# Conformer convolution module: gate tiles, layer-norm root and second product reordered, with the root on GpSimd

## The chip, the cores and the metric

The kernel runs on one core of a Trainium2 chip. The metric is the device time of one execution in microseconds (us), lower is better. Five engines work side by side and meet only at semaphores: TensorE (PE, whose weight loads are PEld), VectorE (DVE), ScalarE (ACT), GpSimd (POOL) and SyncE (SP), which issues the DMAs.

## The reference, cut to what matters

A two-layer hybrid decoder step; only the token mixer of layer 0 is touched, a causal Conformer convolution module over 1,104 tokens (64 of the sample group, 1,040 of the prompt) of width 1,024:

```python
def conformer_conv(h, hist, w_pw1, b_pw1, w_dw, b_dw, ln_g, ln_b, w_pw2, b_pw2):
    u = h @ w_pw1 + b_pw1
    g = u[..., :D_CONV] * jax.nn.sigmoid(u[..., D_CONV:])
    gh = jnp.concatenate([hist.astype(g.dtype), g], axis=1)
    new_hist = gh[:, -CONV_HIST:]
    c = causal_dwconv(gh, w_dw, b_dw)
    c = jax.nn.silu(layernorm(c, ln_g, ln_b))
    return c @ w_pw2 + b_pw2, new_hist
...
    y = xc * lax.rsqrt(jnp.mean(xc * xc, axis=-1, keepdims=True) + EPS)
```

The rest (RMS norms, two SwiGLU feed-forwards, the Mamba-2 mixer of layer 1) is the same in both kernels.

## The kernel before, in words

Tokens lie in three chunks of 368 columns (`TC`, `NC` = 3), model width in eight tiles of 128 (`KT` = 8). A dense product of one output tile and one chunk is 24 matmuls (`dense`: eight k-tiles, each as three fp32r products of high and low parts). Weights come in units of 128 x 1,024 into two slots; ACT splits off the high part (`split`, L1038), POOL the low part (L1763).

**First product (`pw1`).** For each of the eight tiles m there are two units, v = 0 (the linear half, PSUM banks 0 to 2) and v = 1 (the gate, banks 3 to 5). ACT takes the sigmoid chunk by chunk (`gates`, L1105), DVE multiplies (`glu_tile`, L1386 and L1387). PE then turns the finished gate tile of the tile before into rows of time (`turn_gates`, 14 transposes in four sets, through banks 6 and 7), and ACT keeps the four sets in `gt` (`keep_gates`, L1119). Sets 2 and 3 use the same banks as sets 0 and 1, so they wait until ACT has kept those.

**Windows.** The convolution is done by a discrete Fourier transform on 14 windows (`WIN`; 97 tokens each for ten of the prompt and 70 for its last, three small ones of 24, 24 and 16 tokens for the sample group, which come fifth to seventh in `ORDER`). Window x is a step: PE analyses (`analyse`, L664), DVE multiplies by the spectrum of the filter (`products`, L1408 and L1409), PE synthesizes (`synthesize`, L674 and L675), ACT keeps the sums (`keep_sums`, L1128), DVE takes mean and variance (`stats`, L1417 and L1419). PE runs its analysis two windows ahead.

**Layer norm.** ACT takes the root of the variances in three groups (`roots`, L1134: windows 0 to 6, 7 to 9, 10 to 13), DVE inverts it (`inverses`, L1425) and normalises (`normalise`, L1431). PE turns the window back (`turn_back`, 8 transposes), ACT applies gain, bias and silu and splits off the high part (`silus`, L1143 and L1147), POOL the low part (L1793). The table `BEHIND` says behind which step this tail of a window is done: window 0 behind step 7, and only windows 0 to 8 inside the loop of steps.

**Second product (`pw2_first`).** Chunk 0 needs windows 0 to 6, chunk 1 windows up to 9, chunk 2 all; in PE's queue the turns of window 9 and of windows 10 to 13 stand between the chunks. The loop over the other six output tiles follows.

The order of each engine's queue is the order of its block in the code; nothing else schedules.

Of the kernel before, what the change touches and what calls it, by code (L numbers as in the profile page):

```python
# [26 lines left out]
ACT = mybir.ActivationFunctionType  # L27
# [3 lines left out]
P = 128  # L31
# [92 lines left out]
def hybrid_step(nc, i, o):  # L124
    with ExitStack() as ctx:
# [29 lines left out]
        with ExitStack() as conv_scope:  # L155
            def cb(name, shape):
                return conv_scope.enter_context(nc.sbuf_tensor(name, shape, F32))

            wspec = cb("wspec", [P, 2, D])
            tab_k = cb("tab_k", [P, K_END])  # L160
            wrow = cb("wrow", [P, D])
            bst = cb("bst", [P, 2, 12])
            mv = cb("mv", [P, WIN, 2])
            rstd = cb("rstd", [P, WIN])
        ahi = sb("ahi", [P, 2, T], F32R)
# [16 lines left out]
        def chunk_buffer(start):  # L182
# [101 lines left out]
        ws_mm, ws_kept, x_done, t_ready, c_done, c_kept, c_stat = (sem(x) for x in (  # L284
            "ws_mm", "ws_kept", "x_done", "t_ready", "c_done", "c_kept", "c_stat"))
        ln_step, ln_aggr, ln_root, ln_inv, cn_ready, tb_done, y_silu, l_hi, l_lo = (sem(x) for x in (
            "ln_step", "ln_aggr", "ln_root", "ln_inv", "cn_ready", "tb_done", "y_silu", "l_hi", "l_lo"))
# [87 lines left out]
        LN_GROUPS = [(0, 7), (7, 10), (10, WIN)]  # L375
        LN_OF = [n for n, (a, b) in enumerate(LN_GROUPS) for _ in range(a, b)]
        BEHIND = {7: [0], 8: [1], 9: [2], 10: [3], 11: [4, 5], 12: [6, 7], 13: [8]}
# [187 lines left out]
        def _(pe):  # L565
# [65 lines left out]
            def pw1(m):  # L631
                for v in range(2):
                    unit_ready(U_PW1 + 2 * m + v)
                    for c in range(NC):
                        pe.wait_ge(g_glu, NC * m - 2 + c)
                        dense(3 * v + c, v, FULL, xhi, xlo, c)

            def turn_gates(m, a):

                pe.wait_ge(g_glu, NC * m + NC)  # L640
                G = glu[a]
                for n, (w0, w1) in enumerate(SETS):
# [12 lines left out]

            def analyse(x):

                w, n, col, kd, k1, k2 = window(x)
                if x == 4:
                    pe.wait_ge(in_hist, 16 * SWN)  # L660
                for half in range(2):
                    pe.wait_ge(gt_kept, 4 * (3 if half == 0 else 7) + SET_OF[w] + 1)
                    wait(pe, t_ready, 2 * (x - 2) + half + 1)
                    pe.matmul(bank[2 * (x % 2) + half][:, :], tab_k[:, kd:kd + P], gt[:, w, half * 512:half * 512 + 512],  # L664
                              start=True, stop=True).then_inc(x_done, 1)
# [26 lines left out]
            pw1(1)  # L692
            turn_gates(0, 0)
            with pe.Fori(1, KT // 2) as m2:
                pw1(2 * m2)
                turn_gates(2 * m2 - 1, 1)
                pw1(2 * m2 + 1)
                turn_gates(2 * m2, 0)
# [10 lines left out]
            def pw2_first(c):  # L709

                pe.wait_ge(l_lo, (7, 10, WIN)[c])
                for v in range(2):
                    if c == 0:
                        unit_ready(U_PW2 + v)
                    dense(3 * v + c, v, FULL, xhi, xlo, c)
# [317 lines left out]
        def _(act):  # L1033
# [77 lines left out]
            def keep_gates(m):  # L1111

                for n, (w0, w1) in enumerate(SETS):
# [15 lines left out]

            def roots(r):  # L1130

                a, b = LN_GROUPS[r]
                act.wait_ge(ln_aggr, b)
                act.activation(rstd[:, a:b], mv[:, a:b, 1], ACT.Sqrt, bias=eps[:, 0:1]).then_inc(ln_root, 1)  # L1134
# [217 lines left out]
        def _(dve):  # L1352
# [43 lines left out]
            def products(x):  # L1396
# [4 lines left out]
                for half in range(2):  # L1401
                    hs = slice(half * 512, half * 512 + 512)
                    dve.wait_ge(x_done, 2 * x + half + 1)
# [17 lines left out]
            def inverses(r):  # L1421

                a, b = LN_GROUPS[r]
                dve.wait_ge(ln_root, r + 1)
                dve.reciprocal(rstd[:, a:b], rstd[:, a:b]).then_inc(ln_inv, 1)  # L1425

            def normalise(x):

                w, n, col, kd, k1, k2 = window(x)
                dve.wait_ge(ln_inv, LN_OF[x] + 1)  # L1430
# [287 lines left out]
        def _(pool):  # L1718
# [71 lines left out]
            for x in range(WIN):  # L1790
# [3 lines left out]
                                   ALU.subtract).then_inc(l_lo, 1)  # L1794
            for m in range(KT - 2):
# [121 lines left out]
```

## Time and profile before

| what | value |
|---|---|
| median of 3 runs | 3596.91 us (3589.69 to 3606.87) |
| the profiled execution: its time, its span | 3604.03 us, 3602.3 us |
| PE, PEld busy | 3355.0 us (93%), 3180.7 us (88%) |
| DVE, ACT, POOL busy | 1385.1, 894.1, 892.4 us |
| mean granted TensorE clock | 0.969 of full speed |

The span is what the profiler records between the first and the last instruction of the core. PE is busy for nearly all of it, so a change can gain only where PE stands still or runs at its lower clock. The stretch that the change touches lies between 115 and 454 us.

### The profile page before, as it was taken

Reading aid. Unit: us, or ns where it says so; the run is one execution under the profiler, and the core shown is the slowest. Engines: PE = TensorE matmul, PEld = TensorE weight load, DVE = VectorE, ACT = ScalarE, POOL = GpSimd, SP = SyncE. Lnnn points to the kernel's source line nnn. Section 1 sums busy time; section 2 is a strip of 40 time slices with the busy share of each in tenths; the row PEclk is TensorE's granted clock in tenths of the full one; section 3 lists DMA queues with packets and bytes.
Section 4 is the critical chain, followed back from the end, with each engine's and each line's share of the span. In section 5 each row is a group of like instructions: output and inputs, shape, how many; then the busy total and the mean of one; then the engine's idle time right before and its main releaser. Section 6 shows DMA issues by size and latency. Waiting matters only on the chain. (4 is left out here: it accounts for less than half of the span.)

```text
span 3602.3 us, 51683 instructions
## 1 busy us (share of the span) xinstructions
PE 3355.0 (93%) x19814; PEld 3180.7 (88%) x19814; DVE 1385.1 (38%) x2358; ACT 894.1 (25%) x1621; POOL 892.4 (25%) x662
## 2 busy tenths in 40 slices
PE   4999798999999995979999999999987999999998
PEld 3896597999999994969999889999877999999997
DVE  4004323222223236354645556464555222322234
ACT  2212622111111112323333233333322111111112
POOL 2311223121212112323232333333233121121210
PEclk8999899999999997999999999999999999999999
DMA  3111011111111110101111120111110111111111
GB/s 100 36 35 28 1 39 38 42 42 45 41 47 41 47 47 16 42 26 54 38 36 44 44 60 21 54 38 36 48 39 18 48 41 47 41 45 42 44 43 56
DMA packets 226515, 148.43 MB, mean 41 GB/s; under 512 B 7474, under 2 KB 208274, under 8 KB 226320
## 3 DMA queue, kind: packets, MB, share of 16 engines
q1 hardware_dynamic: 226360, 146.31, 13.7%
q8 instruction: 104, 1.70, 0.2%
q14 instruction: 51, 0.42, 0.0%
HBM read 131.56 MB, written 15.44 MB: 41 GB/s over the span
## 5 line engine op out<-in xcount | busy, mean ns | idle before, releaser
L575 PE MATMUL bank<-xhi,whi 128*128 128x368 f32 x3840 | 1293.5, 337 | 94.0 <-issue 33.0
L575 PE MATMUL bank<-xlo,whi 128*128 128x368 f32 x3840 | 1282.9, 334 | 0.0
L575 PE MATMUL bank<-xhi,wlo 128*128 128x368 f32 x3840 | 1279.3, 333 | 0.0
L1763 POOL TENSOR_TENSOR wlo<-stage,whi 128x1024 fp32r<-128x1024 f32 x220 | 537.1, 2442 | 1728.8 <-ACT whi L1038 1728.8
L575 PEld LDWEIGHTS bank<-xhi,whi 128*128 128x128 f32 x3840 | 733.9, 191 | 113.6 <-issue 58.2
L575 PEld LDWEIGHTS bank<-xlo,whi 128*128 128x128 f32 x3840 | 733.1, 191 | 2.7
L575 PEld LDWEIGHTS bank<-xhi,wlo 128*128 128x128 f32 x3840 | 733.1, 191 | 0.0
L1502 DVE TENSOR_TENSOR h<-h,bank 128x368 f32<-128x368 f32 x528 | 284.2, 538 | 720.6 <-PE bank L575 720.6
L575 PE MATMUL bank<-ahi,whi 128*128 128x368 f32 x1440 | 495.2, 344 | 4.3 <-DVE alo L1483 3.8
L575 PE MATMUL bank<-alo,whi 128*128 128x368 f32 x1440 | 477.4, 332 | 0.0
L575 PE MATMUL bank<-ahi,wlo 128*128 128x368 f32 x1440 | 476.9, 331 | 0.0
L1038 ACT ACTIVATE whi<-stage 128x1024 fp32r<-128x1024 f32 x220 | 231.3, 1053 | 587.1 <-PE bank L575 552.6
L575 PEld LDWEIGHTS bank<-ahi,whi 128*128 128x128 f32 x1440 | 271.8, 189 | 8.4 <-DVE alo L1483 4.4
L575 PEld LDWEIGHTS bank<-alo,whi 128*128 128x128 f32 x1440 | 271.8, 189 | 2.7 <-issue 0.3
L575 PEld LDWEIGHTS bank<-ahi,wlo 128*128 128x128 f32 x1440 | 271.6, 189 | 0.0
L1491 DVE TENSOR_TENSOR arena<-arena,bank 128x368 f32<-128x368 f32 x132 | 71.1, 538 | 464.5 <-PE bank L575 464.5
L567 PE MATMUL bank<-ident,arena 128*104 128x128 f32 (+7 forms) x934 | 145.0, 279 | 82.6 <-DVE arena L1666 20.0
L567 PEld LDWEIGHTS bank<-ident,arena 128*104 128x104 f32 (+7 forms) x934 | 107.5, 149 | 113.8 <-issue 40.3
L1199 ACT ACTIVATE ahi<-arena 128x368 fp32r<-128x368 f32 x132 | 67.6, 512 | 446.1 <-DVE arena L1491 446.1
L1608 DVE SCALAR_TENSOR_TENSOR arena<-arena,params 128x1040 f32<-128x1040 f32 x96 | 169.8, 1769 | 0.0
L1187 ACT ACTIVATE arena<-bank 128x368 f32<-128x368 f32 x132 | 62.5, 479 | 398.3 <-PE bank L575 398.2
L1326 ACT ACTIVATE arena<-bank,arena 104x104 f32<-104x104 f32 (+1 forms) x352 | 92.4, 344 | 246.0 <-PE bank L881 245.8
(196 smaller groups left out, 2800.6 us busy)
## 6 DMA issues: line engine op xcount, KB each, us to landing
stage<-in_ssd_w_in SPq DMA_DIRECT2D x48, 512.0 KB, 4.2
stage<-in_ffn_w_gate SPq DMA_DIRECT2D x44, 512.0 KB, 3.8
stage<-in_ffn_w_up SPq DMA_DIRECT2D x44, 512.0 KB, 3.7
stage<-in_ffn_w_down SPq DMA_DIRECT2D x44, 512.0 KB, 3.5
stage<-in_cf_w_pw SPq DMA_DIRECT2D x24, 512.0 KB, 4.0
arena<-in_state_ssm SPq DMA_DIRECT2D x16, 512.0 KB, 4.8
out_ss_s<-arena SPq DMA_DIRECT2D x16, 512.0 KB, 3.2
stage<-in_ssd_w_out SPq DMA_DIRECT2D x16, 512.0 KB, 3.5
```

Source lines behind the costliest of these rows:

```text
L567: return pe.transpose(out, in_, ident[0:k, 0:k])
L575: mm = pe.matmul(bank[b][:, 0:TC], w[:, slot, w0:w0 + P], x[:, k, cs], start=n == 0, stop=n == 3 * len(offs) - 1)
L1038: act.activation(whi[:, slot, :], stage[:, slot, :], ACT.Copy).then_inc(w_hi, 1)
L1187: act.activation(sg[:, j, c * TC:(c + 1) * TC], bank[3 * j + c][:, 0:TC], ACT.Silu)\
L1199: act.activation(ahi[:, j, c * TC:(c + 1) * TC], actv[q % 2], ACT.Copy).then_inc(f_hi, 1)
L1326: a = act.activation(dec[0:l, q * l:(q + 1) * l], bc_bank[0:l, q * l:(q + 1) * l], ACT.Exp, bias=tab[0:l, NACS, c, q:q + 1])
L1491: dve.tensor_tensor(actv[q % 2], sg[:, j, c * TC:(c + 1) * TC], bank[q][:, 0:TC], ALU.mult)\
L1502: dve.tensor_tensor(hm, hm, bank[q % 6][:, 0:TC], ALU.add).then_inc(f_down, 1)
L1608: dve.scalar_tensor_tensor(op, rp[:, t:t + NP_], w, op, ALU.mult, ALU.add).then_inc(r_step, 1)
L1763: pool.tensor_tensor(wlo[:, slot, :], stage[:, slot, :], whi[:, slot, :].bitcast(F32), ALU.subtract)\
```

## The change

Four edits go together. (1) `turn_gates` and `keep_gates` take a list of sets: sets 0 and 1 of the tile before are turned between the two halves of a tile's first product, sets 2 and 3 behind the second half, and the last tile's sets are interleaved with the first analyses (for which `x_done` becomes one semaphore for each half). (2) The root moves from ACT to POOL: `inverse_root` does it for each window by six small operations on a column of one element a partition (add epsilon, power of -0.5, one Newton step), each behind a wait on the one before; ACT's `roots` and DVE's `inverses` are gone. (3) The tail of window x - 1 (normalise, turn back, silu, split) is done behind step x, for all windows. (4) The second product starts behind the loop of steps, with the last window's turn between its first two halves.

```diff
-        LN_GROUPS = [(0, 7), (7, 10), (10, WIN)]
...
-        BEHIND = {7: [0], 8: [1], 9: [2], 10: [3], 11: [4, 5], 12: [6, 7], 13: [8]}
...
-            def pw1(m):
+            def pw1(m, a):
+
                 for v in range(2):
                     unit_ready(U_PW1 + 2 * m + v)
                     for c in range(NC):
                         pe.wait_ge(g_glu, NC * m - 2 + c)
                         dense(3 * v + c, v, FULL, xhi, xlo, c)
-
-            def turn_gates(m, a):
+                    turn_gates(m - 1, a, (2 * v, 2 * v + 1))
+
+            def turn_gates(m, a, sets):
...
-            turn_gates(KT - 1, 1)
-            analyse(0)
-            analyse(1)
+            analyse(0, 0)
+            turn_gates(KT - 1, 1, (0, 1))
+            analyse(1, 0)
+            turn_gates(KT - 1, 1, (2, 3))
+            analyse(0, 1)
+            analyse(1, 1)
             for x in range(WIN):
                 synthesize(x)
                 if x + 2 < WIN:
-                    analyse(x + 2)
-                for y in BEHIND.get(x, ()):
-                    turn_back(y)
+                    analyse(x + 2, 0)
+                    analyse(x + 2, 1)
+                if x:
+                    turn_back(x - 1)
...
-            pw2_first(0)
-            turn_back(9)
+            pw2_first(0, 0)
+            turn_back(WIN - 1)
+            pw2_first(0, 1)
             pe.wait_ge(c_kept, 2 * WIN)
-            pw2_first(1)
-            for x in range(10, WIN):
-                turn_back(x)
-            pw2_first(2)
+            for c in (1, 2):
+                for v in range(2):
+                    pw2_first(c, v)
...
-            gates(1, 1, False)
-            keep_gates(0)
+            keep_gates(0, (0, 1))
+            gates(1, 1, False)
+            keep_gates(0, (2, 3))
             with act.Fori(1, KT // 2) as m2:
-                gates(2 * m2, 0, False)
-                keep_gates(2 * m2 - 1)
-                gates(2 * m2 + 1, 1, False)
-                keep_gates(2 * m2)
-            keep_gates(KT - 1)
+                for a in range(2):
+                    m = 2 * m2 + a
+                    keep_gates(m - 1, (0, 1))
+                    gates(m, a, False)
+                    keep_gates(m - 1, (2, 3))
+            keep_gates(KT - 1, (0, 1, 2, 3))
             for x in range(WIN):
                 keep_sums(x)
-                if x == 6:
-                    roots(0)
-                elif x == 9:
-                    roots(1)
-                for y in BEHIND.get(x, ()):
-                    silus(y)
-            roots(2)
-            for x in range(9, WIN):
-                silus(x)
+                if x:
+                    silus(x - 1)
+            silus(WIN - 1)
...
                 if x + 1 < WIN:
                     products(x + 1)
-                if x in (7, 11):
-                    inverses(x // 8)
-                for y in BEHIND.get(x, ()):
-                    normalise(y)
+                if x:
+                    normalise(x - 1)
                 stats(x)
-            normalise(9)
-            inverses(2)
-            for x in range(10, WIN):
-                normalise(x)
+            normalise(WIN - 1)
...
+            def inverse_root(x):
+
+                w, n, col, kd, k1, k2 = window(x)
+                ve, r0_, sq, e, half_ = (root[0:n, j:j + 1] for j in range(5))
+                pool.wait_ge(ln_aggr, x + 1)
+                rstep(pool.tensor_scalar(ve, mv[0:n, x, 1:2], EPS, None, ALU.add))
+                rstep(pool.tensor_tensor(r0_, ve, half_, ALU.pow))
+                rstep(pool.tensor_tensor(sq, r0_, r0_, ALU.mult))
+                rstep(pool.tensor_tensor(sq, sq, ve, ALU.mult))
+                rstep(pool.tensor_scalar(e, sq, -0.5, 1.5, ALU.mult, ALU.add))
+                pool.tensor_tensor(rstd[0:n, x:x + 1], r0_, e, ALU.mult).then_inc(ln_inv, 1)
...
+            for x in range(WIN):
+                inverse_root(x)
+                if x:
+                    low_part(x - 1)
+            low_part(WIN - 1)
```

**PE, end of the first product.** Before, from the last gate tile's four turns (banks 6 and 7) to the first synthesis:

```order
L567 MATMUL bank6<-ident,arena 127x128 x4
L567 MATMUL bank7<-ident,arena 127x128 x4
L567 MATMUL bank6<-ident,arena 127x128 x3
L567 MATMUL bank7<-ident,arena 24x128 x3
L664 MATMUL bank0<-arena,tab_k 128x512
L664 MATMUL bank1<-arena,tab_k 128x512
L664 MATMUL bank2<-arena,tab_k 128x512
L664 MATMUL bank3<-arena,tab_k 128x512
L674 MATMUL bank4<-arena,tab_k 97x512
```

The same place of the changed kernel (a transpose is L566 there, an analysis L667, the first matmul of a synthesis L677):

```order
L667 MATMUL bank0<-arena,tab_k 128x512
L566 MATMUL bank6<-ident,arena 127x128 x4
L566 MATMUL bank7<-ident,arena 127x128 x4
L667 MATMUL bank2<-arena,tab_k 128x512
L566 MATMUL bank6<-ident,arena 127x128 x3
L566 MATMUL bank7<-ident,arena 24x128 x3
L667 MATMUL bank1<-arena,tab_k 128x512
L667 MATMUL bank3<-arena,tab_k 128x512
L677 MATMUL bank4<-arena,tab_k 97x512
```

The two analyses of the first half (banks 0 and 2) now stand where PE otherwise waits for ACT to empty banks 6 and 7.

**PE, one step of the windows.** Step 1 of the loop in the kernel before, up to the start of step 2:

```order
L674 MATMUL bank4<-arena,tab_k 97x512
L675 MATMUL bank4<-arena,tab_k 97x512
L674 MATMUL bank5<-arena,tab_k 97x512
L675 MATMUL bank5<-arena,tab_k 97x512
L664 MATMUL bank2<-arena,tab_k 128x512
L664 MATMUL bank3<-arena,tab_k 128x512
```

And of the changed kernel (L678 is the second matmul of a synthesis):

```order
L677 MATMUL bank4<-arena,tab_k 97x512
L678 MATMUL bank4<-arena,tab_k 97x512
L677 MATMUL bank5<-arena,tab_k 97x512
L678 MATMUL bank5<-arena,tab_k 97x512
L667 MATMUL bank2<-arena,tab_k 128x512
L667 MATMUL bank3<-arena,tab_k 128x512
L566 MATMUL bank6<-ident,arena 128x97 x4
L566 MATMUL bank7<-ident,arena 128x97 x4
```

The turn of window 0 stands in step 1; before, it stood in step 7.

**POOL, the stretch of the windows.** Before, between the splits of weights (`wlo`) there is only the low part of each window (L1793):

```order
L1763 TENSOR_TENSOR wlo<-stage,whi 128x1024 x14
L1793 TENSOR_TENSOR xlo<-arena,xhi 128x8x97 x4
L1793 TENSOR_TENSOR xlo<-arena,xhi 128x8x24 x2
L1793 TENSOR_TENSOR xlo<-arena,xhi 128x8x16
L1793 TENSOR_TENSOR xlo<-arena,xhi 128x8x97 x6
L1793 TENSOR_TENSOR xlo<-arena,xhi 128x8x70
```

The changed kernel, one window's root and the low part of the window before it (L1796):

```order
L1785 TENSOR_SCALAR root<-mv 97x1
L1786 TENSOR_TENSOR root<-root 97x1
L1787 TENSOR_TENSOR root<-root 97x1
L1788 TENSOR_TENSOR root<-root 97x1
L1789 TENSOR_SCALAR root<-root 97x1
L1790 TENSOR_TENSOR rstd<-root 97x1
L1796 TENSOR_TENSOR xlo<-arena,xhi 128x8x97
```

Six small operations for each of 14 windows (84 in all) now stand in POOL's queue between the low parts.

## Rows read from the trace of the kernel before

**Rows 1.** Windows view: busy us of each engine, PE's granted clock (PEclk), DMA.

```profile
114.79:306.17 191.38, 183.16 (x1093) 180.75 (x1093) 12.91 (x27) 35.36 (x58) 39.12 (x14) 0.99 0.12 36
306.17:316.92 10.75, 8.92 (x38) 5.67 (x37) 2.96 (x6) 5.52 (x10) 2.35 (x1) 0.84 0.13 29
316.92:382.48 65.56, 65.56 (x177) 25.28 (x175) 50.22 (x89) 33.20 (x66) 6.59 (x4) 1.00 0.07 18
382.48:401.49 19.01, 14.89 (x50) 6.67 (x49) 9.62 (x16) 12.64 (x39) 3.47 (x5) 0.73 0.00 1
401.49:453.75 52.26, 35.23 (x194) 33.52 (x193) 7.56 (x13) 24.99 (x59) 12.19 (x8) 0.77 0.00 0
```

**Rows 2.** Groups of instructions, PE, 114.79 to 306.1 us: busy, mean ns | idle before.

```profile
L567 PE MATMUL bank<-ident,arena 128*127 128x128 f32 (+1 forms) x84 | 12.2, 281 | 8.0 <-ACT arena L1119 8.0
```

**Rows 3.** Timeline, PE, one block of gate turns: start, duration, [idle before <- releaser].

```profile
171.08 0.99 PE L567 MATMUL bank<-ident,arena 128*127 128x128 f32 x6 [1.32 <-ACT arena L1119]
```

**Rows 4.** Timeline, ACT, the sets of the last two gate tiles.

```profile
307.91 1.07 ACT L1119 ACTIVATE arena<-bank 127x512 f32 x2
309.34 0.87 ACT L1119 ACTIVATE arena<-bank 127x384 f32 x2 [0.36 <-PE bank L567]
```

**Rows 5.** Timeline, PE, starts of steps 0, 7, 9 and 10, and step 9's parts.

```profile
316.92 1.02 PE L674 MATMUL bank<-arena,tab_k 128*97 128x512 f32 x2
...
353.89 1.02 PE L674 MATMUL bank<-arena,tab_k 128*97 128x512 f32 x2
...
365.53 1.02 PE L674 MATMUL bank<-arena,tab_k 128*97 128x512 f32 x2
...
368.96 1.88 PE L664 MATMUL bank<-arena,tab_k 128*128 128x512 f32 x4
370.68 0.83 PE L567 MATMUL bank<-ident,arena 97*128 97x97 f32 x8
371.35 1.02 PE L674 MATMUL bank<-arena,tab_k 128*97 128x512 f32 x2
```

**Rows 6.** Timeline, DVE, step 9's statistics and what follows them.

```profile
369.56 1.29 DVE L1417 BATCH_NORM_STATS2 bst<-arena 97x6 f32<-97x512 f32 x2 [1.22 <-ACT arena L1128]
370.88 0.21 DVE L1419 BATCH_NORM_AGGREGATE mv<-bst 97x2 f32<-97x12 f32 x1
371.01 0.64 DVE L1408 TENSOR_TENSOR arena<-bank,wspec 128x512 f32<-128x512 f32 x1
...
373.36 0.81 DVE L1431 TENSOR_SCALAR arena<-arena,mv,rstd 97x1024 f32<-97x1024 f32 x1
```

**Rows 7.** Timeline, ACT, one window's silu and the next sums kept.

```profile
365.39 2.70 ACT L1143 ACTIVATE arena<-bank,params 128x97 f32<-128x97 f32 x8 [1.27 <-PE bank L567]
...
368.88 1.06 ACT L1128 ACTIVATE arena<-bank 97x512 f32<-97x512 f32 x2
```

**Rows 8.** Timeline, POOL: small operations of the setup, and one low part.

```profile
5.01 0.31 POOL L1749 TENSOR_TENSOR upto_s<-same_s,upto 64x64 f32<-64x64 f32 x1
5.42 0.24 POOL L1751 TENSOR_SCALAR cut_s<-upto_s 64x64 bf16<-64x64 f32 x1
...
369.06 1.69 POOL L1793 TENSOR_TENSOR xlo<-arena,xhi 128x776 fp32r<-128x776 f32 x1 [4.12 <-ACT xhi L1147]
```

**Rows 9.** Groups of instructions, PE, 316.92 to 453.75 us.

```profile
L575 PE MATMUL bank<-xhi,whi 128*128 128x368 f32 x49 | 18.4, 375 | 11.1 <-POOL xlo L1793 11.1
...
L567 PE MATMUL bank<-ident,arena 97*128 97x97 f32 (+3 forms) x112 | 13.9, 263 | 10.0 <-ACT arena L1143 9.2 <-DVE arena L1431 0.8
```

**Rows 10.** Timeline, DVE: what the second product's chunk 2 releases, half by half.

```profile
449.76 0.60 DVE L1464 SCALAR_TENSOR_TENSOR h<-bank,params,h 128x368 f32<-128x368 f32 x1 [20.63 <-PE bank L575]
453.79 0.60 DVE L1464 SCALAR_TENSOR_TENSOR h<-bank,params,h 128x368 f32<-128x368 f32 x1 [3.43 <-PE bank L575]
```

**Rows 11.** One line of the kernel each: duration ns min/median/max, first and last start.

```profile
L1835 POOL COPY arena<-arena x32: 188/743/752, 1461.6 to 2583.4; 128x3 f32<-128x3 f32 x32
L1431 DVE TENSOR_SCALAR arena<-arena,mv,rstd x14: 758/804/2293, 356.2 to 409.8; 97x1024 f32<-97x1024 f32 x10, 24x1024 f32<-24x1024 f32 x2, 16x1024 f32<-16x1024 f32 x1, 70x1024 f32<-70x1024 f32 x1
```

More of the change, by code:

```diff
@@ L164, in hybrid_step @@
             rstd = cb("rstd", [P, WIN])
+            root = cb("root", [P, 6])
         ahi = sb("ahi", [P, 2, T], F32R)
@@ L283, in hybrid_step @@
         g_sig, g_glu, gt_turned, gt_kept, g_pad = (sem(x) for x in ("g_sig", "g_glu", "gt_turned", "gt_kept", "g_pad"))
[L284 to L287, printed above, removed]
+        ws_mm, ws_kept, t_ready, c_done, c_kept, c_stat = (sem(x) for x in (
+            "ws_mm", "ws_kept", "t_ready", "c_done", "c_kept", "c_stat"))
+        x_done = [sem("x_done0"), sem("x_done1")]
+        ln_step, ln_aggr, rs_step, ln_inv, cn_ready, tb_done, y_silu, l_hi, l_lo = (sem(x) for x in (
+            "ln_step", "ln_aggr", "rs_step", "ln_inv", "cn_ready", "tb_done", "y_silu", "l_hi", "l_lo"))
         res_added = sem("res_added")
@@ L374, in hybrid_step @@
         ORDER = [0, 1, 2, 3] + list(range(PW, WIN)) + list(range(4, PW))
-        LN_GROUPS = [(0, 7), (7, 10), (10, WIN)]
-        LN_OF = [n for n, (a, b) in enumerate(LN_GROUPS) for _ in range(a, b)]
-        BEHIND = {7: [0], 8: [1], 9: [2], 10: [3], 11: [4, 5], 12: [6, 7], 13: [8]}
         SETS = [(0, 4), (4, 8), (8, PW), (PW, WIN)]
@@ L636, in pw1 @@
                         dense(3 * v + c, v, FULL, xhi, xlo, c)
-            def turn_gates(m, a):
+                    turn_gates(m - 1, a, (2 * v, 2 * v + 1))
+            def turn_gates(m, a, sets):
                 pe.wait_ge(g_glu, NC * m + NC)
                 G = glu[a]
-                for n, (w0, w1) in enumerate(SETS):
+                for n in sets:
+                    w0, w1 = SETS[n]
                     if isinstance(m, int) and m == 0:
@@ L654, in turn_gates, with analyse @@
                     mm.then_inc(gt_turned, 1)
-            def analyse(x):
+            def analyse(x, half):
                 w, n, col, kd, k1, k2 = window(x)
+                if x < 2 and half == 0:
+                    pe.wait_ge(g_glu, NC * KT - 2 + 2 * x)
                 if x == 4:
                     pe.wait_ge(in_hist, 16 * SWN)
[L661 to L665, printed above, removed]
+                pe.wait_ge(gt_kept, 4 * (3 if half == 0 else 7) + SET_OF[w] + 1)
+                wait(pe, t_ready, 2 * (x - 2) + half + 1)
+                pe.matmul(bank[2 * (x % 2) + half][:, :], tab_k[:, kd:kd + P], gt[:, w, half * 512:half * 512 + 512],
+                          start=True, stop=True).then_inc(x_done[half], 1)
             def synthesize(x):
@@ L691, in _ @@
             spectra()
-            pw1(1)
-            turn_gates(0, 0)
+            pw1(1, 0)
             with pe.Fori(1, KT // 2) as m2:
[L695 to L698, printed above, removed]
-            turn_gates(KT - 1, 1)
-            analyse(0)
-            analyse(1)
+                pw1(2 * m2, 1)
+                pw1(2 * m2 + 1, 0)
+            analyse(0, 0)
[4 more added lines that the diff above has]
+            analyse(1, 1)
             for x in range(WIN):
@@ L704, in _, with pw2_first @@
                 if x + 2 < WIN:
-                    analyse(x + 2)
-                for y in BEHIND.get(x, ()):
-                    turn_back(y)
-            def pw2_first(c):
+                    analyse(x + 2, 0)
+                    analyse(x + 2, 1)
+                if x:
+                    turn_back(x - 1)
+            def pw2_first(c, v):
                 pe.wait_ge(l_lo, (7, 10, WIN)[c])
[L712 to L715, printed above, removed]
+                if c == 0:
+                    unit_ready(U_PW2 + v)
+                dense(3 * v + c, v, FULL, xhi, xlo, c)
             def pw2(m, a):
@@ L1109, in gates, with keep_gates @@
                 split(2 * m + 3, 1, A_PW1 + 6 * m + 6)
-            def keep_gates(m):
-                for n, (w0, w1) in enumerate(SETS):
+            def keep_gates(m, sets):
+                for n in sets:
+                    w0, w1 = SETS[n]
                     act.wait_ge(gt_turned, 4 * m + n + 1)
@@ L1402, in products @@
                     hs = slice(half * 512, half * 512 + 512)
-                    dve.wait_ge(x_done, 2 * x + half + 1)
+                    dve.wait_ge(x_done[half], x + 1)
                     wait(dve, c_done, 2 * (x - 2) + half + 1)
@@ L1788, in _, with rstep, low_part @@
                 split(2 * m + 3, 1)
-            for x in range(WIN):
+            n_r = [0]
+            def rstep(ins):
+                ins.then_inc(rs_step, 1)
+                n_r[0] += 1
+                pool.wait_ge(rs_step, n_r[0])
+            def inverse_root(x):
[8 more added lines that the diff above has]
+                pool.tensor_tensor(rstd[0:n, x:x + 1], r0_, e, ALU.mult).then_inc(ln_inv, 1)
+            def low_part(x):
                 w, n, col, kd, k1, k2 = window(x)
@@ L1794, in _ @@
                                    ALU.subtract).then_inc(l_lo, 1)
+            rstep(pool.memset(root[:], -0.5))
+            for x in range(WIN):
[3 more added lines that the diff above has]
+            low_part(WIN - 1)
             for m in range(KT - 2):
```

10 lines of the change are left out of this document (1 added, 9 removed).

## The prediction

> **What bounds the kernel now.** The page gives PE 93% of the span, so I read only the stretches where PE is not at work or slow. The windows view cut at the borders of the module shows three [rows 1]: 10.75 us between the last matmul of the first product (306.17) and step 0 of the windows (316.92), with 8.92 busy; then steps 0 to 10, where PE is busy for all of 65.56 us at full clock, so PE itself is the limit; then 382.48 to 453.75, 71.3 us with PE busy for 50.1 and a granted clock of 0.73 and 0.77. The groups view says who is waited for: before 306 us it is ACT emptying the banks of the gate turns, 8.0 us in six blocks [rows 2], 1.32 in each [rows 3]; behind 316.92 it is 11.1 us for POOL's low parts, at the head of chunks 1 and 2 of the second product, and 10.0 us at the turns for ACT's silus [rows 9]. The reader should see that the tail of the windows (normalise, turn, silu, split) starts at step 7 and is then pressed into the last 80 us, while ACT is half idle in steps 0 to 6.
>
> **Gate turns.** Sets 2 and 3 waited because ACT, behind the tile's last sigmoid and a split, had not emptied banks 6 and 7. Now half a tile (three products) lies between the pairs of sets, far more than two keeps of half a microsecond [rows 4]. All six waits go: 8.0 us. The transposes stay; they are only switched to more often, at a price that no row separates, so zero to 0.1 us a block. I take zero.
>
> **Start of the windows.** Call T the end of the last product. ACT's sigmoid and split run until T + 1.74 (307.91) whatever PE does [rows 4], then it keeps tile 6's sets 2 and 3, by T + 2.65. PE turns those sets (0.75), does one half analysis (0.86, half of the 1.72 between 368.96 and 370.68 [rows 5]), waits until T + 2.3 for bank 6, turns tile 7's sets 0 and 1 (until 3.2), second half analysis (4.1), sets 2 and 3 (4.85), two more halves: step 0 starts at T + 6.6, not T + 10.75. But T now holds one more half block of turns, 0.9 us. So this part gives 10.75 - 6.6 - 0.9 = 3.25, and with the 8.0 above **11.2 us**.
>
> **The steps.** PE's parts of a full step are a synthesis of 3.43 us (365.53 to 368.96), an analysis of 1.72 and a turn of 0.67, together 5.82 [rows 5]. Steps 0 to 6 took 36.97 (316.92 to 353.89) without turns; six turns now stand in them, at most 0.67 each: 41.0. Steps 7 to 11 take 5 x 5.82 = 29.1. Steps 12 and 13 have no analysis: 4.1 each, 8.2. Then come six half products of 4.03 (449.76 to 453.79 [rows 10]), 24.2, and the last turn, 0.67.
>
> Does the tail keep up? ACT: a window's silus and split take 365.39 to 368.88, 3.5 us, the sums 1.06 [rows 7]: 4.6 of 5.82. ACT also loses the table loads that each root brought. It keeps the same rhythm as in steps 8 and 9 of before, where one turn a step was done already and PE did not wait. DVE: four products 2.35, normalise 0.81, statistics 1.5 [rows 6]: 4.7 of 5.82. POOL: low part 1.69 [rows 8] and the root. Only behind step 12, which is short, is the tail late: statistics end 5.6 us after the step's start, root 1.7 and normalise 0.8 with handshakes bring the turn of window 12 to 8.4, while PE is through step 13's synthesis at 7.5. One wait of about 1 us. Window 13's chain then lies beside products: chunk 2 needs its low part some 10 us behind PE's first half product and starts 17 us behind it. The 11.1 us before the chunks go.
>
> Sum from step 0: 41.0 + 29.1 + 8.2 + 1.0 + 24.2 + 0.7 = 104.2 us, against 136.9 before (316.92 to 453.79 [rows 5, 10]): **32.7 us**. Some of it is clock: PE stands still no longer than about a microsecond at a time now, and gaps of 1.32 in the first product left the clock there at 0.99 [rows 1, 3], while the stretches with 0.73 and 0.77 are those with long gaps. If it falls once more on the way, a third of what three falls cost in the last stretch, (1 - 0.77) x 52.26 = 12 us at most, so 4 us: lower end.
>
> **The root.** No row shows POOL's power, nor any operation of one element. The nearest: a product of 64 columns starts 0.41 before the next operation, which lasts 0.24 [rows 8]; at 1.69 us for 776 columns the 64 columns make up 0.14. So about 0.28 with its handshake, and six give R = 1.7 us. Lower end six at 0.24, 1.4. Upper end: a copy of three columns lasts 0.188 at best and 0.743 in the middle [rows 11], where DVE runs operations over the same memory; six at 0.85 with the handshake are 5.1. I take 1.7, since DVE's products, which run beside the root, read one operand from PSUM, and ask what R is allowed. The aggregate ends at 371.09, products run until 373.36, so 2.1 us are covered; statistics of the next window start at 369.56 + 5.82 = 375.38, and normalise may end there, so R up to 3.3 delays nobody [rows 6]. Beyond that DVE's loop (R, 0.2 of handshakes, normalise 0.8, statistics 1.5) is longer than 5.82 and each further microsecond costs one in some 12 steps. Power alone may thus take 1.9 us.
>
> A page of the Trainium skill, "GPSIMD Engine Reference", section "Instruction dispatch", says that the first call of freshly loaded code pays some 6 us. Nothing in this trace shows such a load; if the power brought one, the first window's turn alone would come about 4 us late, since later windows find it loaded, and the sum would be 3564.
>
> **Sum.** 3604.03 - 11.2 - 32.7 = 3560.1 us for the profiled execution's own time. That one lies 7.1 above the median of the runs shown; on the median's scale it is 3596.91 - 43.9 = **3553**, which I predict. Behind 454 us nothing changes: the first split for the next tile waits for the same half product, and the loop runs as before.
>
> **Rivals.**
> *The root is the new bound.* At the upper end, R = 5.1, DVE's loop is 7.6 and (5.1 - 3.3) x 12 = 22 us come back: 3575. For it: every operation waits for the one before, and the power is an unknown. Against: 3.3 us are free. 0.17.
> *DVE and POOL block one another.* One normalise lasted 2293 ns where 804 is the median [rows 11], beside a low part. If every normalise met one, DVE's step would be 4.7 + 1.5 = 6.2, 0.4 over PE's, 5 us in all, and the small root operations could be held too: 3558 to 3565. Against: the low part follows the silus, at 3.5 to 5.2 us of a step, normalise stands at 2.0 to 2.8. The page "SBUF — State Buffer" of the Trainium skill, section "SBUF: two separate sides", has the pair of ports that both use locked for a whole instruction, and the 2293 agrees. 0.10.
> *Given back.* PE's gain is lost behind 454 us, because weights of the second product or the nine outputs of the convolution cache, which window 4's products wait for, come late: time within 0.5% of before, 3590. Against: between the last kept gate set and those products lie three steps, 17 us, and the weights were asked for long before. 0.06.
> *Slower.* The power is worked in software one partition after another. At R = 7.0 (power 5.6 us) all 43.9 us are gone; at 8.5 (power 7.1) the kernel is 18 us slower, 3615. It needs an operation that takes ten times any small one in the trace. 0.05.
> *The forecast*, gain 38 to 50 us: 0.62.
>
> **Range and chances.** About 0.5%, 18 us, is what a measurement of this kernel can tell from no change. The forecast's own range is 3547 to 3559; the runs of before spread by 17 us; with the first two rivals and the uncertainty of a median the range is 3538 to 3580. Faster by over 0.5%: 0.89 (forecast, port rival and the root rival). Within: 0.06. Slower: 0.05.
>
> **What the profile would show.** Right: no idle time before the transposes in the first product; 6.6 us instead of 10.75 before step 0; steps of 5.82 from step 1 on with PE busy throughout; no wait for POOL's low parts; a granted clock near 1 until the second product is over; about 104 us from step 0 to the end of chunk 2; the spacing of the root's six operations below 3.3 us. Wrong: steps longer than 5.82 with PE waiting at the turns for DVE's normalise, and behind it a long L1786 on POOL; a late silu; a clock below 0.9; or a gain there and a new wait behind 450 us.

## The result, and the profile after

The changed kernel took 3568.53 us (median of 5 runs, 3559.94 to 3572.17) where the kernel before took 3596.3 in the same comparison: a ratio of 0.9922 [0.9898, 0.9945], or 28 us. The forecast was 3553. With two more copies of the changed kernel (below) there are 17 runs of it, mean 3565.0 ± 1.9 us (± is a standard error throughout), against 3595.9 ± 1.8 for 12 runs of a copy of the kernel before: 31 us. The profiled execution's time was 3567.82, its span 3566.1, its mean granted clock 0.970.

The windows view of the changed kernel, core 0, from the first matmul behind the spectra to the last of the first product, from there to step 0, and from step 0 to the end of chunk 2. The columns are those of [rows 1]: start and end, length, then busy us and number of instructions of PE, PEld, DVE, ACT and POOL, the granted clock, the busy share of the DMA engines and GB/s.

```profile
115.58:297.20 181.62, 181.62 (x1101) 181.33 (x1101) 12.90 (x27) 36.29 (x60) 39.53 (x14) 0.99 0.13 38
297.20:303.79 6.59, 5.91 (x30) 3.56 (x29) 2.58 (x6) 4.18 (x8) 2.40 (x2) 1.00 0.01 3
303.79:408.20 104.41, 103.58 (x418) 58.35 (x417) 65.89 (x115) 62.87 (x156) 44.44 (x99) 1.00 0.05 14
```

PE never stands still in the first stretch, where it lacked 8.2 us before. The second is 6.59 us instead of 10.75 [rows 1]; the third is 104.41 us against 136.9, with 0.83 us of idle time in it and the clock at full speed, where it was 0.73 and 0.77 in the last 71 us [rows 1]. The groups view of PE says the same of the gate turns, 115.58 to 297.20 us: the 8.0 us of [rows 2] are 0.0.

```profile
L566 PE MATMUL bank<-ident,arena 128*127 128x128 f32 (+1 forms) x92 | 12.3, 273 | 0.0
```

PE's timeline: the end of the first product, step 0, the turn of window 0 and the starts of steps 2 and 3 (compare [rows 5]), then the last step with the two last turns.

```profile
297.24 0.82 PE L566 MATMUL bank<-ident,arena 128*127 128x128 f32 x6
297.89 1.02 PE L667 MATMUL bank<-arena,tab_k 128*128 128x512 f32 x2
299.60 1.12 PE L566 MATMUL bank<-ident,arena 128*127 128x128 f32 x8 [0.68 <-ACT arena L1123]
...
303.79 1.02 PE L677 MATMUL bank<-arena,tab_k 128*97 128x512 f32 x2
...
314.09 0.83 PE L566 MATMUL bank<-ident,arena 97*128 97x97 f32 x8
314.76 1.02 PE L677 MATMUL bank<-arena,tab_k 128*97 128x512 f32 x2
...
320.58 1.02 PE L677 MATMUL bank<-arena,tab_k 128*97 128x512 f32 x2
...
378.15 1.05 PE L677 MATMUL bank<-arena,tab_k 128*70 128x512 f32 x2
...
382.61 0.89 PE L566 MATMUL bank<-ident,arena 97*128 97x97 f32 x8 [0.83 <-DVE arena L1419]
...
387.38 0.66 PE L566 MATMUL bank<-ident,arena 70*128 70x70 f32 x8
```

One wait of 0.68 us for bank 6 and one of 0.83 for the turn of window 12 are all the waits in 110 us, and a step with full windows is 5.82 us (314.76 to 320.58). POOL's timeline, the first root and the first low part:

```profile
309.15 0.24 POOL L1785 TENSOR_SCALAR root<-mv 97x1 f32<-97x1 f32 x1 [7.61 <-DVE mv L1413]
309.48 0.58 POOL L1786 TENSOR_TENSOR root<-root 97x1 f32<-97x1 f32 x1
310.13 0.20 POOL L1787 TENSOR_TENSOR root<-root 97x1 f32<-97x1 f32 x1
...
310.97 0.20 POOL L1790 TENSOR_TENSOR rstd<-root 97x1 f32<-97x1 f32 x1
...
318.29 1.70 POOL L1796 TENSOR_TENSOR xlo<-arena,xhi 128x776 fp32r<-128x776 f32 x1 [2.08 <-ACT xhi L1145]
```

The power lasts 0.58 us, and the root is done at 311.17: R = 2.02 us.

**What came back.** At the same DVE instruction late in the second product (510.18 us before, 464.65 after, the 2155th from the end on DVE) the changed kernel is 45.5 us ahead. From there to the end the program is the same in both, and there it loses. I call all that lies before this point, from the last matmul of the spectra, the module, and the rest the stretch behind. The windows view of before: the stretch behind, and in it one group of the Mamba-2 stage of layer 1:

```profile
510.18:3602.30 3092.12, 2927.86 (x17659) 2820.99 (x17657) 1253.42 (x2155) 743.20 (x1352) 778.60 (x594) 0.98 0.14 41
...
1477.36:1555.45 78.09, 69.94 (x443) 63.85 (x442) 30.00 (x52) 25.13 (x56) 26.97 (x25) 0.98 0.17 48
```

The same two stretches after, and 10 us inside the group:

```profile
464.65:3566.10 3101.45, 2937.19 (x17659) 2828.32 (x17657) 1264.37 (x2155) 743.90 (x1352) 778.81 (x594) 0.97 0.14 41
...
1431.41:1516.70 85.29, 77.36 (x443) 69.55 (x442) 29.99 (x51) 25.13 (x56) 26.97 (x25) 0.86 0.16 44
...
1495.20:1505.20 10.00, 8.52 (x43) 7.52 (x42) 2.65 (x7) 2.40 (x9) 1.33 (x3) 0.50 0.00 0
```

The group has 443 matmuls in both, but 7.2 us more in the changed kernel, at a clock of 0.86. The fall is in the last row: from 1495 to 1515 us the granted clock is 0.50 (1.2 GHz) and a matmul takes longer. In the 10 us before it PE was busy for 7.42; in the copy of the same kernel further down, whose clock stayed up, it was busy for 7.45 at the same place.

### The profile page after: what moved, and what is told of

Its sections match the earlier page's. It is cut to its first block and busy times, and to the rows that moved or that the text cites. A ratio compares the mean times of both kernels' runs of the same rounds, so it can differ in the third digit from the quotient of the medians.

```text
span 3566.1 us, 51763 instructions
## 1 busy us (share of the span) xinstructions
PE 3347.1 (94%) x19814; PEld 3178.9 (89%) x19814; DVE 1394.2 (39%) x2355; ACT 886.4 (25%) x1613; POOL 915.0 (26%) x747
## 3 DMA queue, kind: packets, MB, share of 16 engines
q1 hardware_dynamic: 226360, 146.31, 13.9%
## 5 line engine op out<-in xcount | busy, mean ns | idle before, releaser
L566 PE MATMUL bank<-ident,arena 128*104 128x128 f32 (+7 forms) x934 | 142.1, 277 | 66.6 <-DVE arena L1649 20.1
L566 PEld LDWEIGHTS bank<-ident,arena 128*104 128x104 f32 (+7 forms) x934 | 107.8, 147 | 99.4 <-issue 34.3
```

The lines of the kernel that those rows point to most:

```text
L566: return pe.transpose(out, in_, ident[0:k, 0:k])
```

## The experiments

All lengths of the module and of the stretch behind are from the one profile of each kernel, and times are medians of its timed runs; one comparison of each with the kernel before gives the ratio.

**The two halves alone, and each kernel once more.** The first has only the gate sets and the start of the windows:

```diff
-            def pw1(m):
+            def pw1(m, a):
...
+                    turn_gates(m - 1, a, (2 * v, 2 * v + 1))
...
+            analyse(0, 0)
+            turn_gates(KT - 1, 1, (0, 1))
+            analyse(1, 0)
```

> The kernel before with the gate edits alone (sets 0 and 1 of the tile before turned between the halves of a tile's first product, the last tile's turns interleaved with the first analyses); roots, lag and second product as before. Theory A (the parts add, each where it stands): step 0 of the windows starts about 11 us earlier after the first product (idle time before the transposes goes from 9.8 us to under 1), the rest of the module as before, chunk 2 of the second product ends about 11 us earlier; whole kernel 11 us faster, 3585 against 3596. Rival B (the gate edit gains nothing by itself, since PE catches up anyway at the first wait for POOL's low part): the end of chunk 2 moves by less than 4 us.

The second has only the rest: root on GpSimd, tails at a lag of one, the second product behind the loop.

```diff
-                    turn_gates(m - 1, a, (2 * v, 2 * v + 1))
...
+            turn_gates(KT - 1, 1)
+            analyse(0)
+            analyse(1)
```

> The changed kernel with the gate turns and the first analyses as they were before; root on GpSimd, lag of one and early second product stay. Theory A: from step 0 to the end of chunk 2 about 102 to 104 us as in the changed kernel (136.9 before), so chunk 2 ends 33 to 34 us earlier than before; whole kernel 33 us faster if nothing is lost behind the module. Rival C (the 10 us that the changed kernel lost in the Mamba-2 stage come from the tail's part of the change): this kernel too shows a granted clock near 0.86 instead of 0.98 in the first group of the Mamba-2 stage and is only 23 us faster; e1 shows 0.98. Rival D (they are chance of one execution): the clock of that stretch differs between two profiles of one and the same kernel.

The third is the changed kernel again, the fourth the kernel before again, without an edit.

> The changed kernel once more, unedited, for a second profile and more times. Theory A and rival D: chunk 2 of the second product ends at 408 us within 1 us, as in the first profile, while the granted clock of the first group of the Mamba-2 stage (1431 to 1556 us, 0.86 then) differs from the first profile by 0.05 or more, and the distance to the kernel before is 36 us plus or minus 10. Rival C: the clock there is 0.86 again and the stage again 12 us longer than in the kernel before.

> The kernel before once more, unedited, for a second profile. Rival D: the Mamba-2 stage (1402 to 1590 us) has another granted clock than the 0.98 of the first profile, and its length differs by several us, while the convolution module repeats within 1 us (chunk 2 ends at 453.8). Rival C: it repeats too.

| kernel | time us | ratio to before | module | behind |
|---|---|---|---|---|
| before | 3596.3 | | 396.4 | 3092.1 |
| before again | 3595.74 | 0.9995 [0.9982, 1.0007] | 394.1 | 3078.5 |
| gates alone | 3588.06 | 0.9971 [0.9958, 0.9984] | 379.3 | 3095.7 |
| tail alone | 3568.89 | 0.9920 [0.9905, 0.9936] | 362.9 | 3105.4 |
| changed | 3568.53 | 0.9922 [0.9898, 0.9945] | 350.1 | 3101.4 |
| changed again | 3566.79 | 0.9913 [0.9889, 0.9937] | 348.8 | 3087.4 |

Groups views of PE over the first product say whose waits went. With the gates alone, 113 to 300 us:

```profile
L568 PE MATMUL bank<-ident,arena 128*127 128x128 f32 (+1 forms) x100 | 13.5, 274 | 0.7 <-ACT arena L1126 0.7
```

With the tail alone, 113 to 306 us:

```profile
L566 PE MATMUL bank<-ident,arena 128*127 128x128 f32 (+1 forms) x92 | 13.2, 280 | 8.0 <-ACT arena L1117 8.0
```

Each edit removes its own waits and leaves the other's. In the module they are worth 15 to 17 us and 31 to 34 us, and the whole change 44 to 48; the two overlap by about 3 us, which the gates alone gain in the old tail, where the clock fell once less with them. The time does not follow: the gates alone gain 8.6 us (10.8 ± 2.1 in the means), and on top of the tail they are worth 13 us in the module but 5.9 ± 2.9 in the time. The copies show two things. One program's profiles differ by 14 us behind the module (3101.4 and 3087.4, 3092.1 and 3078.5) while the module repeats to 2.3 us. And the mean behind is longer in the changed kernel. The windows view of its copy, the same stretches as above:

```profile
462.78:3550.20 3087.42, 2924.08 (x17659) 2817.37 (x17657) 1264.01 (x2155) 743.59 (x1352) 778.82 (x594) 0.98 0.14 41
...
1428.68:1506.73 78.05, 69.97 (x443) 63.80 (x442) 29.99 (x51) 25.13 (x56) 26.97 (x25) 0.98 0.17 48
...
1492.50:1502.50 10.00, 7.04 (x53) 6.08 (x52) 4.53 (x12) 2.68 (x10) 2.80 (x5) 0.92 0.00 0
```

The same program, and the group is back at 78.05 us, its clock at 0.98. So the 85.29 is not fixed by the program, neither by POOL's new work nor by the order of anything; what differs between the two executions is the clock. With the tail alone the group is 85.30 us and its clock 0.86, with the gates alone 78.06 and 0.98.

**Is the root on GpSimd needed, and what may it cost?** First the root back on ACT, still window by window, with everything else as changed:

```diff
+            def root_of(x):
+                w, n, col, kd, k1, k2 = window(x)
+                act.wait_ge(ln_aggr, x + 1)
+                act.activation(rstd[0:n, x:x + 1], mv[0:n, x, 1:2], ACT.Sqrt, bias=eps[0:n, 0:1]).then_inc(ln_root, 1)
...
+                if x:
+                    root_of(x - 1)
                 keep_sums(x)
...
+                dve.wait_ge(ln_root, x + 1)
+                dve.reciprocal(rstd[0:n, x:x + 1], rstd[0:n, x:x + 1]).then_inc(ln_inv, 1)
```

> The changed kernel with the root back on ScalarE, now for each window (square root behind the previous window's silus, reciprocal on VectorE before the normalise); lag, gate turns and second product as changed. Theory A (the root had to leave ScalarE for the lag of one to pay): two table loads of 1.28 us and the root of 0.3 come to each window, so ScalarE needs 3.5 + 1.06 + 2.9 = 7.4 us a window where PE needs 5.8; steps 2 to 11 take about 7.4 us, step 0 to the end of chunk 2 takes 104 + 10 x 1.6 = 120 us or a little more, the kernel is about 16 us slower than the changed one, 3583. Rival (the move is worth nothing, the lag alone does it): 104 us again.

It took 3598.84 us, ratio 1.000 [0.9988, 1.0012]: the whole gain is gone. ACT's timeline over one step of it:

```profile
324.83 1.28 ACT L1138 ACT_TABLE_LOAD   x1
326.12 0.29 ACT L1138 ACTIVATE rstd<-mv,eps 97x1 f32<-97x1 f32 x1
326.32 1.06 ACT L1132 ACTIVATE arena<-bank 97x512 f32<-97x512 f32 x2
328.16 1.28 ACT L1147 ACT_TABLE_LOAD   x1 [0.77 <-PE bank L566]
329.46 2.69 ACT L1147 ACTIVATE arena<-bank,params 128x97 f32<-128x97 f32 x8
332.18 0.85 ACT L1151 ACTIVATE xhi<-arena 128x776 fp32r<-128x776 f32 x1
333.05 1.28 ACT L1138 ACT_TABLE_LOAD   x1
```

A step lasts 8.22 us (324.83 to 333.05) instead of 5.82: ACT's own work adds up to 7.45, of which the two table loads (root, silu and back) are 2.56, and 0.77 is its wait for the turn. The module is 380.1 us, 30 over the changed kernel's, more than the 16 expected; the longer waits of PE bring falls of its clock too (at 345, 383, 400 and 417 us). The module is then no shorter than with the gates alone (379.3), so with one square root a window on ACT the new tail gives nothing. Moving the root is thus no side edit. A root for two windows at a time on ACT, or a root on DVE, was not tried.

Then a longer root, by dependent multiplications ahead of its last operation, 12 and 4 of them:

```diff
+                for _ in range(12):
+                    rstep(pool.tensor_tensor(root[0:n, 5:6], sq, ve, ALU.mult))
                 pool.tensor_tensor(rstd[0:n, x:x + 1], r0_, e, ALU.mult).then_inc(ln_inv, 1)
```

> The changed kernel with twelve more small dependent products on GpSimd in each window's root, whose results nobody reads; each starts 0.28 us after the one before, so the root takes 2.0 + 3.4 = 5.4 us. Theory A (3.3 us are free, and beyond that each microsecond costs one in a full step): steps grow to R + 2.5 = 7.9 us, 2.1 over PE's 5.8, some 12 times: step 0 to the end of chunk 2 takes about 104 + 25 = 129 us. Rival (the root is covered by the lag whatever it takes): 104 to 108 us.

> The changed kernel with four more small dependent products in each root, R = 3.1 us. Theory A: below the 3.3 us that are free, so steps stay at 5.8 us and the stretch from step 0 to the end of chunk 2 at 105 us (plus 1 us behind window 12, whose chain is not covered). Rival (what e6 showed already begins here, since its steps were 3.6 us longer than the root and not 2.5): steps of 6.7 us, some 10 us more.

With 12 more, R is 5.3 us and the time 3606.44, ratio 1.0023 [1.0009, 1.0036]; the module is 392.2 us, 42 over, where 25 was expected, its steps up to 9.59 us, and the clock falls seven times in its steps and the chunks behind them. Its timeline of POOL and DVE between two aggregates:

```profile
375.82 0.21 DVE L1413 BATCH_NORM_AGGREGATE mv<-bst 97x2 f32<-97x12 f32 x1
...
376.12 0.22 POOL L1785 TENSOR_SCALAR root<-mv 97x1 f32<-97x1 f32 x1 [2.07 <-DVE mv L1413]
...
381.32 1.69 POOL L1798 TENSOR_TENSOR xlo<-arena,xhi 128x776 fp32r<-128x776 f32 x1
381.41 2.15 DVE L1419 TENSOR_SCALAR arena<-arena,mv,rstd 97x1024 f32<-97x1024 f32 x1 [3.02 <-POOL rstd L1792]
383.48 1.27 DVE L1411 BATCH_NORM_STATS2 bst<-arena 97x6 f32<-97x512 f32 x2
...
384.79 0.21 DVE L1413 BATCH_NORM_AGGREGATE mv<-bst 97x2 f32<-97x12 f32 x1
```

The loop of 8.97 us (375.82 to 384.79) is 0.30 to POOL, 5.29 of root, 2.07 of normalise and 1.31 of statistics. Normalise costs 0.8 us alone; here POOL's low part, which had waited in the queue behind the root, starts 0.09 us ahead of it, and it lasts 2.15. The section "SBUF: two separate sides" of the page "SBUF — State Buffer" in the Trainium skill has whichever of the two starts first hold the shared pair of ports for its whole instruction. The trace agrees nearly: normalise ends 0.55 us behind the low part, a little less than the 0.8 it would need if it began only then. The reverse is there too: behind window 12 of the changed kernel normalise starts 0.31 us ahead, keeps its 0.8 us, and the low part lasts 2.08 instead of 1.69. Where the starts lie closer the recorded order does not decide, since the normalise of 2293 ns in the kernel before [rows 11] starts 0.06 us ahead of the low part. So two of the rivals are one once the root is late: a root that sets the pace starts the low part and normalise at the same moment.

With 4 more, R is 3.1 us and the time 3565.03, ratio 0.9919 [0.9895, 0.9943]: no different from the changed kernel. Steps 0 to 11 are as long as there, as the allowance of 3.3 us said. From step 0 to the end of chunk 2 it is 108.9 us, where 106 at most was expected, and the module is 4.3 us longer, all of it from step 12 on. Its timeline there:

```profile
381.95 1.69 POOL L1798 TENSOR_TENSOR xlo<-arena,xhi 128x776 fp32r<-128x776 f32 x1
382.04 2.15 DVE L1419 TENSOR_SCALAR arena<-arena,mv,rstd 97x1024 f32<-97x1024 f32 x1 [3.19 <-POOL rstd L1792]
...
384.25 0.89 PE L566 MATMUL bank<-ident,arena 97*128 97x97 f32 x8 [2.84 <-DVE arena L1419]
```

In the short steps the two meet again, and PE waits 2.84 us there and 1.82 at the last turn, instead of 0.83 and nothing.

**Where the other 15 us went.** The claim was now that the module keeps its gain and that the stretch behind pays for being started at another moment. To move that moment and as little else as possible, 3 or 16 transposes that nobody reads stand behind the module (16 take 1.7 us, by the 0.65 for six in the timeline above), in the changed kernel behind the last half product of `pw2_first`:

```diff
+            for k in range(16):
+                turn(bank[6][:, (k % 4) * P:(k % 4 + 1) * P], ident[:])
```

> The changed kernel with three transposes of the identity into a free bank, read by nobody, behind the second product's first two tiles: PE's later work starts 0.32 us later. Theory E (since the module no longer ends with a fall of PE's clock, whose recovery set the start of all later work in the same way in every execution, the later stages begin at an instant that is free relative to the clock's changes, and in most executions it is an unlucky one by a few tenths of a us): 0.3 us later is luckier, the granted clock lost behind the module falls by 8 to 12 us, the kernel gets faster, about 3557 instead of 3567, and the first group of the Mamba-2 stage shows 0.98 instead of 0.86. Theory D (chance alone, the same for all kernels): 3567 plus or minus 4.

> The changed kernel with sixteen such transposes, PE's later work 1.7 us later. Theory E: the start then stands where e2 had it relative to the clock's changes, so nearly every execution has the low clock in the first group of the Mamba-2 stage: 3570 to 3574, none below 3560. Theory D: 3568 plus or minus 4, with the same spread as the changed kernel (3550 to 3574).

and 16 in the kernel before, at the same place:

> The kernel before with the sixteen transposes of e8 at the same place, behind the second product's first two tiles (1.7 us of PE's work, read by nobody). Theory E: in the kernel before, the last fall of the clock inside the module sets the start of the later work, to an instant that is lucky for the Mamba-2 stage in every profile so far; 1.7 us later it is an unlucky one, so the first group shows 0.86 instead of 0.98 as in e8, 7 us longer, and the kernel is slower by more than the 1.7 us, about 3603 against 3596. Theory D (chance alone): 3598.

The kernel with 3 was then timed again, and the changed one a third time:

> e7 once more, for a second profile and more times. Theory E: the first group of the Mamba-2 stage again at 78 us, median 3556 to 3562. Theory D: 3567 plus or minus 4, the group at 78 or 85 us by chance.

> The changed kernel a third time. Both theories: the convolution module as in the first two profiles within 0.3 us. Theory E: times spread between 3550 and 3574 with most above 3564, median 3567; the stage's first group at 85 us if PE reaches the feed-forward at an unlucky instant. Theory D: no difference to e11.

| kernel | time us | ratio to before | module | behind |
|---|---|---|---|---|
| changed, 3 more | 3561.39 | 0.9897 [0.9880, 0.9915] | 350.4 | 3094.4 |
| the same again | 3561.70 | 0.9910 [0.9889, 0.9932] | 349.1 | 3094.0 |
| changed, 16 more | 3570.74 | 0.9922 [0.9905, 0.9939] | 350.5 | 3105.2 |
| before, 16 more | 3607.54 | 1.0032 [1.0019, 1.0045] | 397.0 | 3100.7 |
| changed, third | 3566.95 | 0.9911 [0.9888, 0.9934] | 350.2 | 3105.1 |

The clearest is the fourth row. Sixteen transposes of 1.7 us made the kernel before 12 us slower: 3607.9 ± 1.5 over 12 runs against 3595.8 ± 1.4 over 17. In the changed kernel 16 against 3 are 8.5 ± 2.7 us in the means, of which 1.4 are the transposes themselves. The modules of the changed kernel with 3 and 16 are within 1.4 us, that of the kernel before with 16 is 397.0 beside 396.4 and 394.1, and the program behind is the same. But the mark by which I meant to know it failed once: I had tied the loss to the first group of the Mamba-2 stage. It is 78.1 us in both profiles with 3 more and 85.3 with 16 more, as expected, but in the kernel before with 16 more it is 77.98 us; there the next one was longer (37.77 instead of 34.73), and others behind. The group with 16 more and with 3 more, in the changed kernel:

```profile
1429.26:1514.55 85.29, 77.23 (x443) 69.56 (x442) 29.99 (x52) 25.13 (x56) 26.97 (x25) 0.86 0.16 44
...
1431.24:1509.33 78.09, 69.95 (x443) 63.86 (x442) 30.00 (x51) 25.13 (x56) 26.96 (x25) 0.98 0.17 48
```

All fourteen profiles of these kernels fall in two kinds by this group and in nothing between. Five have 85.28 to 85.30 us at a clock of 0.86 (the changed kernel's first and third, the tail alone, 16 more, the root on ACT), and their stretch behind is 3101.4 to 3105.4 us. Nine have 77.98 to 78.09 at 0.98, with 3078.5 to 3100.7 behind. All five have the new tail, as ten of the fourteen do, which can be chance.

The times say something else that one pair of kernels hides. The mean time less the module is 3200.7 us for the kernel before, and between 3207.2 and 3219.9 for all nine other programs, 3210.9 for the kernel before with 16 more (each to some 3 us). So the kernel before is the lucky one in its later stages, rather than the changed one the unlucky.

One instruction behind does last longer in the changed kernel: a copy on DVE at the head of each of the eight groups of the Mamba-2 stage, 2.05 us instead of 0.28 in six of them. The groups views of DVE, before and after, without the first group:

```profile
L1583 DVE COPY arena<-arena 104x200 f32 x7 | 2.0, 284 | 22.4 <-issue 21.3 <-POOL arena L1881 1.1
...
L1566 DVE COPY arena<-arena 104x200 f32 x7 | 12.6, 1793 | 8.0 <-POOL arena L1891 8.0
```

It is not the loss: wait and copy together are 20.6 us instead of 24.4, so it is done earlier, and the kernels with 3 more, with R at 3.1 and with R at 5.3 have it too and are at 3092 to 3094 us behind. Why the wait turned into a longer copy is open. That 3 transposes help at all is not shown: 3561.9 ± 1.5 over 11 runs against 3565.0 ± 1.9 over 17 differ by 3.1 ± 2.4. With that reserve it is the fastest kernel measured here, 3561.4 us.

## Why the prediction was right in sign and range, and 15 us low

**Gate turns and start of the windows: right in mechanism, a little low.** 11.2 us were forecast for both. From the first matmul of the product to step 0 it was 202.1 us [rows 1] and is 188.2 (115.58 to 303.79), so 13.9, and 13.1 between the means of the two profiles of before and the three of after. All 8.0 us of waits went, and 6.6 us before step 0 were forecast where 6.59 were measured. The 2 us more lie in the product, where PE is busy for less although half a block of turns was added; no run says why. The 0.1 us a block that I left out for switching is not there.

**The steps: right.** 104.2 forecast, 104.41 measured: 32.7 and 32.5 us. The wait of "about 1 us" at the turn of window 12 is 0.83, the one place where DVE is waited for, and no chunk waits for POOL. One reading was wrong without effect: the lower end divides 12 us of clock by three falls, but the stretch from 401.49 to 453.75 us has two, so a fall costs 6 us and not 4; none came.

**The root: a price a little low, without effect.** R was put at 1.7 us, all six operations at 0.28 apart. Four spacings are 0.28 to 0.33; the one behind the power, which itself takes 0.58, is 0.65, and the root is 2.02. The allowance of 3.3 us covered it. It held in the long steps at 3.1 us, and beyond it the price was too small, since every long step with a late root also pays 1.3 us for the low part: 42 us in the module with R at 5.3 instead of the 22 of the rival at 5.1. The first call's 6 us of the Trainium skill (page "GPSIMD Engine Reference", section "Instruction dispatch") are not seen: the first power of the program lasts 0.58 us, the second 0.57, and the first root 2.02, the second 1.98. The 3564 that the forecast would have been with them stands on the scale of the profiled execution; on the forecast's own scale it is 3557.

**The sum: here it failed.** The step is "Behind 454 us nothing changes". As far as orders, waits and outputs go that held. In the granted clock it did not: the stretch behind is 3092.1 and 3078.5 us in the two profiles of the kernel before and 3101.4, 3087.4 and 3105.1 in the three of the changed one, 12.7 longer in the mean. The last of the changed kernel, in the windows view:

```profile
461.39:3566.50 3105.11, 2942.20 (x17659) 2834.07 (x17657) 1264.21 (x2155) 743.51 (x1352) 778.26 (x594) 0.97 0.14 41
```

and the second of the kernel before:

```profile
506.58:3585.10 3078.52, 2916.47 (x17659) 2809.62 (x17657) 1252.66 (x2155) 742.73 (x1352) 778.15 (x594) 0.98 0.14 41
```

The same 17,659 matmuls of PE are busy for 25.7 us more in the first; these two lie furthest apart. The modules are 395.2 and 349.7 in the mean, 45.6 apart; less 12.7 that is 33, and the timed runs say 31. So the module gave the 43.9 that were forecast and a bit more, and a quarter to a third of it was lost behind.

**What of that is shown, and what is open.** Shown: 1.7 us of PE's work ahead of the stretch behind cost 12 us, with the module and the program behind unchanged; in the profiles the loss sits in the granted clock; it isn't bound to this program, since one program's profiles fall on either side. Argued, not shown: that the moment of the start does it, since no run moves the start without adding instructions, which also puts all later ones 16 places further on. Not shown: why later groups of the Mamba-2 stage lose their clock from the changed kernel's start more often than from the old one's. With 5 profiles the 12.7 could in part be the draw; the 31 us of the timed runs, against 45.6 in the module, could not.

**The rivals.** The root as the new bound did not come, but was one experiment away (R = 5.3 costs more than the whole gain). The port rival did not come: normalise lasts 791 to 815 ns in all 14 windows, since the low part never starts ahead of it; where it starts 0.31 us behind, at window 12, the low part is the one that waits. The estimate of a step of 6.2 us was harmless beside what it does together with a late root. "Given back" had the right place and the wrong means: no weight and no output is late. Slower did not come.

## What to carry to other kernels

Where PE is the bound, let the work that follows it keep up one step behind instead of in a tail; here it turned 71 us at three quarters of the clock into work at full clock. Before that, count what each engine must do in one step and in the shortest step, table loads and port conflicts included, since one engine over the step (ACT at 8.22, DVE at 8.97 instead of 5.82) gives everything back. And take a gain of 1% in the early part of a kernel with a stretch behind it whose clock comes and goes as uncertain by some 10 us, until the kernel has been measured with that stretch moved by a few matmuls.

## What the runs showed of the hardware that was not expected

- A power on one element a partition on GpSimd takes 0.57 to 0.58 us, other operations of that size 0.19 to 0.24, and each one that waits for such a one before it starts 0.28 to 0.33 us behind it, 0.65 behind a power.
- 1.7 us of matmuls that nobody waits for made a kernel 12 us slower; its profile shows the missing granted clock in several stages of the 3,100 us behind them.
- One group of 443 matmuls takes 78.0 to 78.1 us or 85.3 us and nothing between in fourteen profiles, at a granted clock of 0.98 or 0.86.
- Two executions of one program differ by 14 us behind the same point, by the clock alone: PE is busy for 13.1 us more (2937.19 and 2924.08) and the other engines within 0.4 us.
